# Queries, keys and probabilities of the first block's heads turned by transposing DMAs that ScalarE begins

## What is computed

```
h  = rmsnorm(x); q, k, v of 8 "dilated" heads (A) and 8 "differential" heads (B) = h @ w_in
A: s = q k^T * 128**-0.5 + log(count of windows that see the key);  y = softmax(s) v
B: p0 = softmax(q0 k0^T), p1 = softmax(q1 k1^T);  y = rmsnorm((p0 - lam * p1) v) * gain
x += [yA, yB] @ w_out;  x += (silu(g @ w_gate) * (g @ w_up)) @ w_down  with g = rmsnorm(x)
```

## Time and profile before

| | |
|---|---|
| median of 3 runs | 2502.57 us (2502.16 to 2503.18) |
| the profiled execution | 2502.62 us, its span 2500.8 us |
| PE busy | 2488.7 us (100%) |
| DVE, ACT, POOL busy | 1454.7, 1222.2, 459.8 us |
| DMA, mean | 199 GB/s |
| TensorE clock granted | 9 tenths or more in every slice |

### The profile page before, as it was taken

How to read it: one execution, slowest core, us unless ns; L and a number is a source line. 1 busy time by engine, 2 the same in 40 slices (tenths; PEclk the granted TensorE clock), 3 DMA queues, 4 the chain that set the end, 5 groups by cost and what they waited for, 6 DMA issues and landing times.

```text
span 2500.8 us, 30691 instructions
## 1 busy us (share of the span) xinstructions
PE 2488.7 (100%) x11196; PEld 2057.6 (82%) x11196; DVE 1454.7 (58%) x1723; ACT 1222.2 (49%) x1666; POOL 459.8 (18%) x411
## 2 busy tenths in 40 slices
PE   9999999999999999999999999999999999999999
PEld 7878888888888888888888888888888888888887
DVE  5655556555555555565455555566567646675665
ACT  6554445444344434455445544544555535553553
POOL 2433212111011101131000110112233103320330
PEclk9999999999999999999999999999999999999999
DMA  9776667776677667676666666667777767866775
GB/s 241 186 182 174 175 190 206 202 209 201 195 202 204 207 194 202 201 228 194 180 186 176 182 182 186 179 189 217 208 213 210 216 194 219 219 209 194 204 216 185
DMA packets 433425, 497.34 MB, mean 199 GB/s; under 512 B 128832, under 2 KB 231844, under 8 KB 433184
## 3 DMA queue, kind: packets, MB, share of 16 engines
q1 hardware_dynamic: 431952, 493.52, 68.3%
q0 software_dynamic: 1088, 2.07, 0.3%
q10 hardware_dynamic: 272, 0.26, 0.0%
HBM read 467.44 MB, written 2.11 MB: 188 GB/s over the span
## 4 chain that ended last, share of the span: by engine, by line
PE 98%; SPq 0%; DVE 0%; ACT 0%; DMA 0%; issue 0%; POOL 0%; ACTq 0%; POOLq 0%
PE ps L546 32%; PE ps L548 32%; PE ps L547 32%; PE ps L656 1%; PE ps L641 0%; PE ps L629 0%; DMA raw<-in_w_in 0%; PE ps L732 0%; PE ps L714 0%; PE ps L792 0%; PE ps L937 0%; PE ps L623 0%; ACT w_hi L1008 0%; SPq L491 0%; SPq L444 0%
## 5 line engine op out<-in xcount | busy, mean ns | idle before, releaser
L1427 DVE TENSOR_TENSOR w_lo<-raw,w_hi 128x1024 fp32r<-128x1024 f32 x880 | 1116.8, 1271 | 1000.3 <-ACT w_hi L1008 997.4
L1008 ACT ACTIVATE w_hi<-raw 128x1024 fp32r<-128x1024 f32 x880 | 930.6, 1059 | 1156.0 <-PE ps L548 1086.0
L546 PE MATMUL ps<-w_hi,xT_hi 128*128 128x512 f32 x2204 | 870.5, 395 | 0.8 <-DVE xT_lo L1446 0.8
L548 PE MATMUL ps<-w_hi,xT_lo 128*128 128x512 f32 x2204 | 859.3, 390 | 0.0
L547 PE MATMUL ps<-w_lo,xT_hi 128*128 128x512 f32 x2204 | 858.2, 389 | 0.0
L546 PE MATMUL ps<-w_hi,yT_hi 128*128 128x512 f32 x1312 | 512.3, 390 | 0.0
L548 PE MATMUL ps<-w_hi,yT_lo 128*128 128x512 f32 x1312 | 510.7, 389 | 0.0
L547 PE MATMUL ps<-w_lo,yT_hi 128*128 128x512 f32 x1312 | 510.6, 389 | 0.0
L546 PEld LDWEIGHTS ps<-w_hi,xT_hi 128*128 128x128 f32 x2204 | 413.9, 188 | 87.1 <-issue 2.7
L548 PEld LDWEIGHTS ps<-w_hi,xT_lo 128*128 128x128 f32 x2204 | 413.6, 188 | 87.0
L547 PEld LDWEIGHTS ps<-w_lo,xT_hi 128*128 128x128 f32 x2204 | 414.1, 188 | 83.6
(11 more groups left out here) (215 smaller groups left out, 883.9 us busy)
## 6 DMA issues: line engine op xcount, KB each, us to landing
raw<-in_w_up SPq DMA_DIRECT2D x264, 512.0 KB, 4.3
raw<-in_w_down SPq DMA_DIRECT2D x176, 512.0 KB, 4.4
raw<-in_w_in SPq DMA_DIRECT2D x160, 512.0 KB, 3.8
raw<-in_w_gate SPq DMA_DIRECT2D x88, 512.0 KB, 4.3
raw<-in_w_out SPq DMA_DIRECT2D x60, 512.0 KB, 3.9
raw<-in_w_in SPq DMA_DIRECT2D x128, 192.0 KB, 3.2
raw<-in_w_in SPq DMA_DIRECT2D x192, 128.0 KB, 2.6
raw<-in_w_proj_m SPq DMA_DIRECT2D x16, 512.0 KB, 4.0
```

The lines of the kernel that those rows point to most:

```text
L546: pe.matmul(o, hi[:, q], w_hi[n % NS][:, k, 0:width], start=first, stop=False)
L548: mm = pe.matmul(o, lo[:, q], w_hi[n % NS][:, k, 0:width], start=False, stop=last)
L1008: nc.scalar.activation(w_hi[n % NS][:, :, 0:width], raw[n % NS][:, :, 0:width], ACT.Copy).then_inc(hi_ready, 1)
L1427: v.tensor_tensor(w_lo[n % NS][:, :, 0:width], raw[n % NS][:, :, 0:width], f32(w_hi[n % NS][:, :, 0:width]), ALU.subtract).then_inc(lo_rea ...
```

## The change

The steps of the heads are renumbered. A head now starts at unit 14 + 6k, PE's turn of the probabilities and ACT's copy of them are gone, and the product with the values is at step 7. In their place POOL writes the probabilities as 16-bit halves (`halve_p`), ACT starts a transposing DMA of them at step 4 (`P_SENT`, unit 18 + 6k), and POOL joins the turned halves to `pT` (`join_p`). The transposing DMA of q and k is now started by ACT as well, at step -2 (unit 12 + 6k), no longer by SP. For q and k of head k+1 that is the same unit 18 + 6k, so ACT starts the two one behind the other. SP waits for all of them once, before its first x turn. The seven `late` loads are spread over units 24 to 30. ACT's `heads_out` (the copies of finished banks) goes ahead of `heads` in a unit. The last head ends at unit 112, so `out_a` also calls `heads`. Buffers for the halves are unused parts of `z1` and `z2`.

```diff
-HEAD_STEPS = (1, 4, 5, 8)
-HEAD_FIRST, HEAD_EVERY = 13, 6
-QK_SENT = 3
+DIFF_STEPS, DIL_STEPS = (1, 7, 11), (1, 7, 8)
+HEAD_FIRST, HEAD_EVERY = 14, 6
+QK_SENT, P_SENT = -2, 4
...
+        p_bufs = [across_bufs(z2[:, 1, C3 // 2:C3 // 2 + 4 * S]), across_bufs(z1[:, 1, 0:4 * S])]
         qkT_halves = qkT[:, :, :].rearrange("p c s -> p (c s)").bitcast(U16).rearrange("p (f t s e) -> p f t s e", f=2, t=NT, e=2)
+        pT_halves = pT.bitcast(U16).rearrange("p (f t s e) -> p f t s e", f=2, t=NT, e=2)
...
-            def turn_heads(unit):
-                k = sent_at(unit, QK_SENT)
-                if k is not None:
-                    sp.wait_ge(qk_halved, k + 1)
-                    split_, flipped_ = qk_bufs[k // HEADS]
-                    sp.dma_start_transpose(flipped_.rearrange("p t e f s -> p (t e f) s"),
-                                           split_.rearrange("p t e n -> p (t e n)")).then_inc(qk_across, 16)
             def load(n, i, step, src, width):
                 sp.wait_ge(lo_ready, at(i, n + 1, step))
                 sp.dma_start(raw[n % NS][:, :, 0:width], src).then_inc(raw_landed[n % NS], 16)
-                turn_heads(n + i * step)
                 if n + i * step - AHEAD in SENT:
                     k = SENT[n + i * step - AHEAD]
+                    if k == 0:
+                        sp.wait_ge(qk_across, 2 * HEADS * 16)
+                        sp.wait_ge(p_across, 2 * HEADS * 16)
...
-            heads_in("in_b", C3, lambda u: load_x(u + 1) if u < 7 else None)
-            for dst, src in late:
-                sp.dma_start(dst, src).then_inc(late_landed, 16)
+            def x_or_late(u):
+                if u < 7:
+                    load_x(u + 1)
+                if LATE_FROM <= u < LATE_FROM + N_LATE:
+                    dst, src = late[u - LATE_FROM]
+                    sp.dma_start(dst, src).then_inc(late_landed, 16)
+            heads_in("in_b", C3, x_or_late)
             heads_in("in_a", 0)
...
-                u_scores, u_p, u_values, u_y = HEAD_STEPS
-                if u == u_p:
-                    pe.wait_ge(hb.mixed, h.upto(2))
-                    turn_p(hb, mix, FULL_SRC)
...
-                u_scores, u_p, u_values, _ = HEAD_STEPS
-                if u == u_p:
-                    pe.wait_ge(ha.mixed, h.upto(2))
-                    turn_p(ha, prob, FULL_SRC)
...
-            residual("out_a", 4, yT, 0, KT, ready=lambda u: pe.wait_ge(ha.y_lo, FREE + UK * (u + 1)))
+            residual("out_a", 4, yT, 0, KT, first=lambda u: heads(112 + u), ready=lambda u: pe.wait_ge(ha.y_lo, FREE + UK * (u + 1)))
...
-                    p_out(ha, h, 2 * S)
+                u_scores, _, u_y = DIL_STEPS
                 if u == u_scores:
+                    act.wait_ge(p_halved, h.upto(1, HEADS))
                     act.wait_ge(ha.row_max, h.upto())
...
+            def turned_across(k, bufs, halved_, across_):
+                split_, flipped_ = bufs[k // HEADS]
+                act.wait_ge(halved_, k + 1)
+                act.dma_start_transpose(flipped_.rearrange("p t e f s -> p (t e f) s"),
+                                        split_.rearrange("p t e n -> p (t e n)")).then_inc(across_, 16)
             def heads(unit):
                 for kind, head, u in heads_at(unit):
                     (diff_head, dil_head)[kind](u, Head(0, head, 0))
+                k = sent_at(unit, QK_SENT)
+                if k is not None:
+                    turned_across(k, qk_bufs, qk_halved, qk_across)
+                k = sent_at(unit, P_SENT)
+                if k is not None:
+                    turned_across(k, p_bufs, p_halved, p_across)
...
                 def behind(u):
+                    heads_out(u, "in_a", i, z2)
                     heads(48 + 16 * i + u)
-                    heads_out(u, "in_a", i, z2)
...
                     dve.wait_ge(hb.coef, h.upto())
+                    dve.wait_ge(p_halved, h.num())
...
+                    dve.wait_ge(p_halved, HEADS)
...
+            def halve_p(k):
+                s, head = (hb, ha)[k // HEADS], k % HEADS
+                pool.wait_ge(s.mixed, 2 * (head + 1))
+                g_.tensor_copy(p_bufs[k // HEADS][0], (mix_halves, prob_halves)[k // HEADS]).then_inc(p_halved, 1)
+            def join_p(k):
+                s, head = (hb, ha)[k // HEADS], k % HEADS
+                pool.wait_ge(p_across, 16 * (k + 1))
+                pool.wait_ge(hb.pv, min(k, HEADS))
+                if k > HEADS:
+                    pool.wait_ge(ha.pv, head)
+                g_.tensor_copy(pT_halves, p_bufs[k // HEADS][1].rearrange("p t e f s -> p f t s e")).then_inc(s.pT, 1)
...
-            for k in range(2 * HEADS):
-                if k < HEADS - 1:
-                    rope_head(hb, Head(0, k + 1, 0), "in_b", z1, rope_b, 2, 16)
-                elif k < 2 * HEADS - 1:
-                    if k == HEADS - 1:
-                        pool.wait_ge(late_landed, 16 * N_LATE)
-                    rope_head(ha, Head(0, k + 1 - HEADS, 0), "in_a", z2, rope_a, 1, 32)
-                if k < 2 * HEADS - 1:
-                    halve_qk(k + 1)
+            def rotate(k):
+                if k < HEADS:
+                    rope_head(hb, Head(0, k, 0), "in_b", z1, rope_b, 2, 16)
+                elif k < 2 * HEADS:
+                    pool.wait_ge(late_landed, 16 * N_LATE)
+                    rope_head(ha, Head(0, k - HEADS, 0), "in_a", z2, rope_a, 1, 32)
+                if k < 2 * HEADS:
+                    halve_qk(k)
+            def values_in(k):
                 if k >= HEADS:
                     h = Head(0, k - HEADS, 0)
                     if k == HEADS:
                         pool.wait_ge(hb.y_T, HEADS)
                     pool.wait_ge(by_act, evacuated("in_a", h.first, V_GROUPS))
                     stage_v(ha, h, z2, h.num(WH, 2 * P))
+            for k in range(2 * HEADS):
+                rotate(k + 1)
+                if 1 <= k <= HEADS:
+                    head_factor(hb, Head(0, k - 1, 0), NT, 2, eps_diff)
+                halve_p(k)
+                values_in(k)
                 if k < 2 * HEADS - 1:
                     join_qk(k + 1)
-                if k < HEADS:
-                    head_factor(hb, Head(0, k, 0), NT, 2, eps_diff)
+                join_p(k)
```

More of the change, by code:

```diff
@@ L111 @@
 QK_GROUPS, V_GROUPS = (1, 2, 2, 3), (1, 2, 3, 3)
-N_SMALL, N_LATE = 14, 7
+N_SMALL, N_LATE, LATE_FROM = 14, 7, 24
 WARM = (6, 5)
@@ L164, in heads_at, with sent_at @@
     return [(k // HEADS, k % HEADS, unit - HEAD_FIRST - k * HEAD_EVERY) for k in range(2 * HEADS)
[L165 to L171, removed]
+            if 0 <= unit - HEAD_FIRST - k * HEAD_EVERY <= DIFF_STEPS[-1]]
+def sent_at(unit, step):
+    k = (unit - HEAD_FIRST - step) // HEAD_EVERY
+    return k if 0 <= k < 2 * HEADS and HEAD_FIRST + k * HEAD_EVERY + step == unit else None
 def evacuated(name, head, groups):
@@ L273, in two_blocks @@
         turned = work[:, 8 * S:12 * S].rearrange("p (f s) -> p f s", s=S)
-        stage_halves = work[:, 10 * S:12 * S].bitcast(U16).rearrange("p (t n e) -> p t e n", t=NT, e=2)
+        stage_halves, mix_halves, prob_halves = (work[:, c * S:(c + 2) * S].bitcast(U16).rearrange("p (t n e) -> p t e n", t=NT, e=2)
+                                                 for c in (10, 4, 0))
         turned_halves = work[:, 8 * S:12 * S].bitcast(U16).rearrange("p (n e) -> p n e", e=2)
@@ L363, in two_blocks @@
         stored, half_done = sem("stored"), sem("half_done")
-        hb = HeadSems(sem, "diff", ("masked", "v_staged", "qk_T"))
-        ha = HeadSems(sem, "dil", ("raw_max", "coef", "sq", "ms", "rstd", "y", "y_T", "qk_T", "y_coef"))
+        hb = HeadSems(sem, "diff", ("masked", "v_staged", "qk_T", "p_T"))
+        ha = HeadSems(sem, "dil", ("raw_max", "coef", "sq", "ms", "rstd", "y", "y_T", "qk_T", "p_T", "y_coef"))
         hm = HeadSems(sem, "mlstm", ("rope", "v_staged", "y_coef"))
@@ L669, in _ @@
             FULL = {(t, kt): 2 * kt + t for t in range(NT) for kt in range(2)}
-            FULL_SRC = [t * S + kt * P for kt in range(2) for t in range(NT)]
             CAUSAL = {(0, 0): 0, (1, 0): 1, (1, 1): 2}
@@ L724, in dil_head @@
             def dil_head(u, h):
-                u_scores, u_p, u_values, _ = HEAD_STEPS
-                if u == u_p:
-                    pe.wait_ge(ha.mixed, h.upto(2))
-                    turn_p(ha, prob, FULL_SRC)
+                u_scores, u_values, _ = DIL_STEPS
                 if u == u_scores:
@@ L1078, in diff_head @@
             def diff_head(u, h):
-                u_scores, u_p, u_values, u_y = HEAD_STEPS
-                if u == u_p:
-                    p_out(hb, h, 2 * S)
+                u_scores, u_values, u_y = DIFF_STEPS
                 if u == u_scores:
@@ L1129, in behind @@
                     nc.scalar.activation(lam_t[:, 2:4], lam_t[:, 0:2], ACT.Exp).then_inc(lam_exp, 1)
+                heads_out(u, "in_b", 0, z1)
                 heads(u)
-                heads_out(u, "in_b", 0, z1)
```

(8 more changed lines are left out.)

9 lines of the change are left out of this document (3 added, 6 removed).

## The result

The changed kernel took 2524.62 us (median of 4 runs, 2521.52 to 2527.51) beside 2502.36 us for the kernel before (4 runs, 2501.39 to 2503.18). The ratio is 1.0089, with a 95% interval of 1.0077 to 1.0101: 22 us slower, where 12 us faster had been forecast. The profiled execution took 2521.52 us, with a span of 2519.7 us. It is the case that stands as rival 3 in the prediction, with a chance of 0.07 and a time of 2526 us.

The account below looks back on a forecast made before the run. The prediction took PE's work plus PE's waits to bound the kernel. 7.3 + 3.3 + 1.7 + 0.7 - 1.0 = 12.0 us off 2502.6 gave 2490.6 us, with a range of 2487.5 to 2497.5 us.

Parts of the forecast that it names:

- rival 3: Slow ACT starts and landings make PE wait 2.3 us in each of 16 heads: 2526 us; chance 0.07.
- the landing of the probabilities: ACT's two transposing DMAs: probabilities landed 5.1 us after the first start, at T + 6.3 or T + 5.2.
- the new path: Probabilities through DMA and POOL's join: ready T + 7.5, wanted T + 8.2, 0.7 us to spare; 1.0 us allowed.
- the 0.7 us of the blocks: Values of head k and scores of head k+1 in one block, 15 times: 0.7 us gained, middle of 0 and 1.4.
- Turns 7.3: PE's turns of the probabilities go: 0.455 us per turn of a head, 7.3 us gained over 16 heads.
- the 3.3 us wait: PE's single wait for DVE at a head's turn of probabilities, about 159.4 to 162.68, goes: 3.3 us gained.
- 1.7 us for the two at the values: PE's two waits for POOL at the product with the values go: listed 1.3 us, counted 1.7 us gained.
- rival 2: The 3.3 us stall only moves: ACT waits for POOL's halves, PE starves; 2493.9 us, up to 2497; chance 0.12.
- T: The moment at which PE ends unit 18 + 6k, from which the new path's times are counted.
- ACT's start: First transposing DMA starts at T + 1.2 behind ACT's 1.06 us split, or T + 0.1 if it need not wait.
- `join_p`: POOL's join of the turned probabilities: 1.17 us at the median, 2.74 at most, ending T + 7.5, up to T + 9.0.
- The clock: In the heads the granted clock stays at 1.00, its upper level of 2.4 GHz; no PE idling long enough for another.

## Why the prediction was wrong

The step that failed is the landing of the probabilities on the new path: it was taken at 5.1 us after ACT's first start, from a pair on SP, and came at 7.2 us at head 2 and 7.6 us at the median of the 15 pairs. The terms for PE stood up, but for the 0.7 us of the blocks.

**The terms for PE held.** Turns 7.3, the 3.3 us wait and 1.7 us for the two at the values: 2502.6 - 12.3 + 0.8 for the one wait that is left is 2491.1 us. The kernel with SP's starts and later values took 2491.2 and 2491.4. In it, no wait of the earlier trace rows has come back. So rival 2 fell: no kernel in which DMAs turn the probabilities has a wait of PE for DVE in the heads.

**Blocks together, 0.7 us: worth nothing.** In the rows of the swapped joins, the merged block without a wait takes 2.62 us from L546 before it to L545 behind it, less the two plain steps of 0.455 a price of 2.17 us. In the kernel before, the values cost 0.9 us, as the prediction has it, and the scores 1.26 on the same count (130.07 to 131.78). Nothing was saved.

```profile
130.07 0.39 PE L548 MATMUL ps<-w_hi,xT_lo 128*128 128x512 f32 x1
...
131.78 0.40 PE L547 MATMUL ps<-w_lo,xT_hi 128*128 128x512 f32 x1
```

**The new path, step by step** (head 2):

- ACT's start: forecast T + 1.2, or T + 0.1 at the early end. It was T + 0.02. This end of the bounds was right and gave 1.2 us of spare time.
- The landing: forecast 5.1 us after the first start. It was 7.2, from 108.60 to 115.75. This is the step that failed, and with it the sentence "these two are in another queue, so I take the pair's value". A slow landing on SP was read as a fault of SP's queue. The runs show the reverse: the queue behind the loads is what gave 3.6 us, and the other queue gives 5.3 to 6.1 in the eight kernels that use it beside whole loads.
- `join_p`: forecast 1.17, up to 2.74. It took 1.88 at head 2 and 1.3 at the median. It is long where it starts while a `w_lo` of DVE (L1428) is running: 1.25 to 2.16 us at the nine heads of that kind (here a `w_lo` ran from 115.39 to 116.62), 1.15 or 1.16 at the other seven.
- So T + 9.05, where PE wanted it at T + 8.2. A wait of 0.81 us, and 13 more of them.

Rival 3 had the place right, an entry at the values in nearly every head. Its size was too large, 37 us, where 21.9 us in 14 waits came, 1.6 us each; the clock, below, made up for a part of that. Its reason was the landing; its other part, a start of 2.03 us each time, came only in small part (medians of 1.25 us for the first of a pair and 1.63 for the second). Its chance of 0.07 rested on the median of SP as the value for ACT. With a landing bounded by 3.6 and 7.3 us and a spare time of 0.7, half of that range lay past the point where the change loses.

**The clock.** That "nothing in the change would leave PE idle long enough to expect another" level was wrong. Busy time of PE in 20 us stretches of the changed kernel (window; sum, busy, matmuls; granted clock; DMA share; GB/s):

```profile
320.00:340.00 20.00, 16.00 (x66) 0.91 0.77 191
340.00:360.00 20.00, 18.61 (x75) 0.92 0.55 116
360.00:380.00 20.00, 17.43 (x70) 0.91 0.54 157
```

and in steps of 2 us, with PE's two long waits:

```profile
334.00:336.00 2.00, 0.00 (x0) 1.00 0.91 298
336.00:338.00 2.00, 0.60 (x2) 0.64 1.04 381
338.00:340.00 2.00, 2.00 (x6) 0.50 0.61 221
340.00:342.00 2.00, 2.00 (x6) 0.50 0.03 8
...
344.00:346.00 2.00, 2.00 (x11) 1.00 0.00 0
```

```profile
337.40 2.08 PE L654 MATMUL ps<-work 128*128 128x256 f32 x4 [4.00 <-POOL work L2043]
...
362.57 1.13 PE L654 MATMUL ps<-work 128*128 128x256 f32 x4 [3.95 <-POOL work L2043]
```

Behind each of the two waits, of heads 13 and 14, the granted clock is 0.50, the lower level of 1.2 GHz, and six matmuls fit where eleven did. Over the three stretches this is (0.09 + 0.08 + 0.09) x 20, some 5.2 us of time at full speed. The first fall came at 336.6, while PE still waited, so that some 0.4 us of it cost nothing, and 4.8 us were lost. Not the length of the wait alone decides. In this and the other runs the clock fell around waits of 4.46, 4.00, 3.99, 3.95, 3.58 and 2.51 us, in the run with the earlier start alone also around one of 2.02 and one of 1.85 and in that with swapped joins and later values around one of 1.99, and not around the 3.3 us of the earlier trace rows or the 2.43 at 139.14 here. The runs don't show what does. The DMA share of 0.91 to 1.04 in the first wait shows how busy the engines were that the transpose shared with the loads.

**The account of the profiled run.** 2502.6 - 12.3 + 22.7 (waits) + 4.8 (clock in the heads) + 1.3 is 2519.1 us, against 2521.52. The 1.3 us are at the start, where the first bank was written at 36.72 instead of 35.41, with 3.4 us at the lower clock from 8.9 us on; the change does not touch that stretch. The 2.4 us left are near what entering a block after a wait costs on top of what the list books, 0.24 us in the earlier trace rows, at 15 waits at most 3.6; that is an estimate.

**What stays open.** Why the landings of heads 13 and 14 are the longest, 9.5 and 9.4 us. They lie in `out_b`, and in the run with quarter loads, which ends with `in_a`, these heads still waited 3.99 and 3.58 us. That fits the sharing of the engines, but smaller loads in `out_b` were not tried. Of the 2.4 us that ACT's queue costs, the parts ahead of the first and behind the last packet were not explained. And POOL's joins were not swapped with ACT's starts left as they were, so the 32 us below are not split between the two edits.

## What to carry to other kernels

Before a DMA is moved off a busy queue, read what its place in that queue gave it: in SP's queue, among loads, it ran with 30 to 74 KB of their bytes in between; beside them it took over 2 us longer. A path with 0.7 us to spare and an unmeasured row of 3.6 to 7.3 us in it is a coin toss, so the first run should give it slack (values a unit later, or the consumer's join first in its engine's order) and then take the slack away. And where two steps are put in another order, put in the same order every engine they pass: ACT's earlier start was worth 7 us alone and 32 us with POOL's joins swapped.

## What the runs showed of the hardware

- A transposing DMA of 256 KB that ACT begins beside SP's weight loads lands 5.3 to 6.1 us after its start (median), begun by SP behind the loads 3.6 to 3.9, and begun by ACT beside loads of a quarter 3.8 (one run).
- ACT's DMA start is not held by the activation in front of it: split at 108.58, start at 108.60 (103.68 and 103.71 in the run with fewer transposes).
- Around single waits of PE of 1.85 to 4.46 us the granted clock went to its lower level for 3.4 or 6.8 us, in the changed kernel and in four others; around others of 1.89, 2.17, 2.43 and 3.29 us it stayed at 1.00. So a wait can cost up to nearly twice what the list books (1.85 us, and half of 3.4 on top).
- POOL's copy of 128x1024 16-bit values takes 1.04 us for the halves and 1.15 us for the joins, and up to 1.97 and 2.16 us where it starts while a `w_lo` of DVE is running; where the `w_lo` starts second, POOL's copy keeps its time and the `w_lo` takes longer (1.23 us alone, 2.22 beside the join at 137.89).
